# Gated DeltaNet sample step: state products moved from TensorE to VectorE, keys and queries broadcast through memory

## What is computed

```python
def sample_step(S, q, k, v, decay, beta):        # what the chunked rule comes to for one token
    delta = beta * (v - decay * (k @ S))         # 128 values
    S_new = decay * S + outer(k, delta)          # 128 x 128
    o = (q * 128 ** -0.5) @ S_new
    return o, S_new
```

## Time and profile before

| | us |
|---|---|
| median of three runs | 1199.55 |
| the three runs | 1198.0, 1199.55, 1202.51 |
| the profiled execution, its time | 1204.32 |
| the profiled execution, its span in the trace | 1202.5 |

### The profile page before, as it was taken

The page is one execution under the profiler, slowest core; times in us unless marked ns, Lnnn a source line. Parts: engine busy times, 40 slices in busy tenths (PEclk is TensorE's granted clock), DMA queues, the critical chain, the costliest instruction groups (busy, mean ns, idle before and its releaser), DMA issues. The chain is left out here.

```text
span 1202.5 us, 24731 instructions
## 1 busy us (share of the span) xinstructions
PE 1165.9 (97%) x8401; PEld 1087.4 (90%) x8401; DVE 801.4 (67%) x1987; ACT 475.1 (40%) x1216; POOL 307.2 (26%) x275
## 2 busy tenths in 40 slices
PE   5999999999999999999999999999999979999997
PEld 4899989998999899989988999899999979999996
DVE  5586567666766786777766766777776756565544
ACT  6453335434533444344434433453345335331211
POOL 0224112411242134122311241223122312222211
PEclk9999999999999999999999999999999999999999
DMA  7332455254525452635263525352535373423263
GB/s 249 93 98 73 145 158 162 72 165 147 168 64 177 136 162 62 203 110 166 67 193 108 168 66 194 116 161 81 182 111 168 93 251 129 150 88 101 73 212 143
DMA packets 83354, 164.18 MB, mean 137 GB/s; under 512 B 12801, under 2 KB 22882, under 8 KB 81698
## 3 DMA queue, kind: packets, MB, share of 16 engines
q1 hardware_dynamic: 81966, 161.47, 42.5%
q10 hardware_dynamic: 1312, 1.59, 0.5%
HBM read 144.78 MB, written 17.37 MB: 135 GB/s over the span
## 5 line engine op out<-in xcount | busy, mean ns | idle before, releaser
L643 PE MATMUL PJ<-h,w_hi 128*128 128x512 f32 x1110 | 419.3, 414 | 0.0
L1995 POOL TENSOR_TENSOR w_lo<-w_raw,w_hi 128x512 fp32r<-128x512 f32 x160 | 216.2, 1352 | 758.5 <-ACT w_hi L1035 758.1
L639 PE MATMUL PJ<-h,w_hi 128*128 128x264 f32 (+1 forms) x1216 | 358.0, 294 | 0.0
L640 PE MATMUL PJ<-h,w_hi 128*128 128x264 f32 (+1 forms) x1216 | 345.7, 284 | 0.0
L641 PE MATMUL PJ<-h,w_lo 128*128 128x264 f32 (+1 forms) x1216 | 345.4, 284 | 0.0
L644 PE MATMUL PJ<-h,w_lo 128*128 128x256 f32 x1110 | 311.3, 280 | 0.0
L643 PEld LDWEIGHTS PJ<-h,w_hi 128*128 128x128 f32 x1110 | 209.2, 188 | 42.8 <-DVE w_lo L1397 1.4
L640 PEld LDWEIGHTS PJ<-h,w_hi 128*128 128x128 f32 x1216 | 230.4, 189 | 2.2
L1035 ACT ACTIVATE w_hi<-w_raw 128x512 fp32r<-128x512 f32 x320 | 196.5, 623 | 86.4 <-PE PJ L641 79.1
L639 PEld LDWEIGHTS PJ<-h,w_hi 128*128 128x128 f32 x1216 | 230.0, 189 | 0.3
L641 PEld LDWEIGHTS PJ<-h,w_lo 128*128 128x128 f32 x1216 | 229.0, 188 | 0.0
(11 more groups left out here) (333 smaller groups left out, 1705.8 us busy)
## 6 DMA issues: line engine op xcount, KB each, us to landing
w_raw<-in_w_in SPq DMA_DIRECT2D x256, 256.0 KB, 2.7
w_raw<-in_w_out SPq DMA_DIRECT2D x64, 256.0 KB, 3.0
kvq<-in_cache_win_k SPq DMA_DIRECT2D x24, 512.0 KB, 5.0
kvq<-in_cache_win_v SPq DMA_DIRECT2D x24, 512.0 KB, 4.8
mem<-scratch_p SPq DMA_DIRECT2D x24, 512.0 KB, 5.7
out<-memx SPq DMA_DIRECT2D x16, 260.0 KB, 4.0
mem<-in_x_prompt SPq DMA_DIRECT2D x4, 1024.0 KB, 10.1
S<-in_state_delta SPq DMA_DIRECT2D x8, 512.0 KB, 5.8
```

The source lines that it names most:

```text
L639: pe.matmul(ps, wh, h_hi[:, k, tok], start=k == 0, stop=False)
L640: pe.matmul(ps, wh, h_lo[:, k, tok], start=False, stop=False)
L643: pe.matmul(both, wh, h2[:, :, k, tok], start=k == 0, stop=False)
L1995: pool.tensor_tensor(w_lo[:, par, 4 * q:4 * q + 4, :], w_raw[:, q, :, :], w_hi[:, par, 4 * q:4 * q + 4, :].bitcast(F32), ALU.subtract).the ...
```

## The change

The states are kept with the value dimension on the partitions and the key dimension along the row (the host transposes input and output; the DMAs keep their sizes). Then k @ S is a product along the row, and for that each partition needs the whole of k and of q of every sample:

- DVE transposes the samples' k columns into `qrow` in slot 15, SP writes them to memory with four small DMAs (`rows_to`) in slot 16 and reads them back in slot 19 as a broadcast to all partitions, `k_rows` (which lies in `gx`), 512 KB. The same for q: DVE slot 33, SP slot 35, broadcast to `q_rows` in slot 38.
- DVE does 8 fused multiply-and-sum instructions for k @ S in the slots 35 and 36, six small ones for delta in slot 37, 8 multiply-adds of 128 x 128 into `S0` in the slots 41 to 43, 8 fused ones for q @ S_new in the slots 44 to 47, and two small ones in slot 48. The last two follow in slot 51.
- PE keeps the sum of squares (slot 35, 16 columns) and the sum of o squared (slot 49). L910, L916 and L928 go. POOL keeps the scaling of `S0`, L2059 goes; so do L1747, L1748, L1763 to L1781 in their old form and L1795 on DVE, and one copy on ACT.
- The load of the first key block moves from slot 51 to slot 52, ahead of the q row's broadcast in the same slot; the products with the values on DVE move from the slots 47 to 50 to the slots 48 to 51.

```diff
             def attn_rows(h):
...
-                yield from idle(51)
+                yield from idle(52)
                 if not first:
                     sp.wait_ge(s["pv_ok"], h)
                 keys(0)
-                yield
-                sp.wait_ge(s["qrow_out"], 64 * h + 64)
+                sp.wait_ge(s["qrow_out"], 192 * h + 192)
                 sp.dma_start(qb[:], scratch_q[h].rearrange("b d -> (b d)").partition_broadcast(P)).then_inc(s["qb_in"], 16)
...
             # SP
             def delta_decode(h):
-                yield from idle(24)
+                yield from idle(16)
+                sp.wait_ge(s["q_row"], 3 * h + 1)
+                rows_to(scratch_dk[h])
+                yield from idle(3)
+                sp.wait_ge(s["qrow_out"], 192 * h + 64)
+                sp.dma_start(k_rows, scratch_dk[h].rearrange("b d -> (b d)").partition_broadcast(P)).then_inc(
+                    s["dk_in"], 16)
+                yield from idle(5)
                 if not isinstance(h, int) or h > 0:
                     sp.wait_ge(s["S0_out"], 16 * h)
+                    sp.wait_ge(s["d_vec"], h)
                 sp.dma_start(S0[:], state_delta[h]).then_inc(s["S0_in"], 16)
-                yield from idle(23)
-                sp.wait_ge(s["d_add"], 2 * h + 2)
-                sp.dma_start(st_s[0, :, h].rearrange("b d e -> d b e"), S0[:]).then_inc(s["S0_out"], 16)
+                yield from idle(11)
+                sp.wait_ge(s["q_row"], 3 * h + 2)
+                rows_to(scratch_dq[h])
+                yield from idle(2)
+                sp.wait_ge(s["d_ks"], h + 1)
+                yield
+                sp.wait_ge(s["qrow_out"], 192 * h + 128)
+                sp.dma_start(q_rows[:], scratch_dq[h].rearrange("b d -> (b d)").partition_broadcast(P)).then_inc(
+                    s["dq_in"], 16)
+                yield from idle(9)
+                sp.wait_ge(s["d_add"], h + 1)
+                sp.dma_start(st_s[0, :, h].rearrange("b e d -> e b d"), S0[:]).then_inc(s["S0_out"], 16)
...
             # PE
             def delta_decode(h):
...
-                pe.matmul(MD[:, 1, 0:24], ones[:], dd[:, 2:5, :].rearrange("p a b -> p (a b)"), start=True, stop=True)
-                for b in range(NB):
-                    last = pe.matmul(MD[:, 1, 32 + 2 * b:34 + 2 * b], S0[:, b, :], dd[:, 0:2, b], start=True,
-                                     stop=True)
+                pe.matmul(MD[:, 1, 0:16], ones[:], dd[:, 2:4, :].rearrange("p a b -> p (a b)"), start=True,
+                          stop=True).then_inc(s["d_sum"], 1)
+                yield from idle(14)
                 pe.wait_ge(s["d_vec"], h + 1)
-                for i in range(2):
-                    pe.transpose(MD[0:4 * NB, 1, i * P:(i + 1) * P], kv4[:, i, :], ident[:])
...
-                    pe.matmul(MD[:, 1, :], kvr_all[:, 0, :], vexp_all, start=True,
-                              stop=True).then_inc(s["d_outer"], 1)
...
             # DVE
+            def fused(x, rows, out, acc_, per):
+                for b in range(NB):
+                    last = dve.tensor_tensor_reduce(out=out[:, b * P:(b + 1) * P], in0=S0[:, b, :],
+                                                    in1=rows[:, b * P:(b + 1) * P], scale=1.0, scalar=0.0, op0=ALU.mult,
+                                                    op1=ALU.add, accum_out=acc_[:, b:b + 1])
+                    if b + 1 in per:
+                        yield
...
             def delta_decode(h):
...
+                dve.wait_ge(s["dk_in"], 16 * h + 16)
+                dve.wait_ge(s["S0_in"], 16 * h + 16)
+                yield from fused(s["d_ks"], k_rows, q_rows, dd[:, 0], (5,))
...
+                dve.wait_ge(s["S0_scaled"], h + 1)
+                for b in range(NB):
+                    last = dve.scalar_tensor_tensor(S0[:, b, :], k_rows[:, b * P:(b + 1) * P], dd[:, 4, b:b + 1],
+                                                    S0[:, b, :], ALU.mult, ALU.add)
+                    if b in (2, 4):
+                        yield
+                last.then_inc(s["d_add"], 1)
...
+                dve.wait_ge(s["dq_in"], 16 * h + 16)
+                yield from fused(None, q_rows, q_rows, dd[:, 1], (3, 5, 6))
...
-            def attn_decode(hh, late=0, gap=31, each=2):
+            def attn_decode(hh, late=0, gap=32, each=2):
```

More of the change, by code:

```diff
@@ L491, in conv_out, with rows_to @@
                     yield from idle(8)
+            def rows_to(scratch):
+                for i in range(HD // 32):
+                    sp.dma_start(scratch[:, 32 * i:32 * i + 32], qrow[32 * i + 32 - NB:32 * i + 32, :]).then_inc(
+                        s["qrow_out"], 16)
             def attn_out(h):
                 yield from idle(47)
[L496 to L499, removed]
+                sp.wait_ge(s["q_row"], 3 * h + 3)
+                rows_to(scratch_q[h])
                 yield from idle(6)
@@ L1287, in delta_decode @@
                 rsqrt(dd[:, 9:11, :], MD[:, 1, 0:2 * NB].rearrange("p (a b) -> p a b", a=2), 1.0, s["d_rs"])
[L1288 to L1292, removed]
+                yield from idle(13)
+                act.wait_ge(s["d_sq"], h + 1)
+                rsqrt(dd[:, 10, :], MD[:, 1, 16:24], 1.0 / HD, s["d_rs2"])
             def attn_decode(hh, late=0):
@@ L1539, in own_a @@
                 dve.wait_ge(s["q_ok"], h + 1)
-                if not first:
-                    dve.wait_ge(s["qrow_out"], 64 * h)
+                dve.wait_ge(s["qrow_out"], 192 * h + 128)
                 dve.transpose(qrow[:], xa[:, TT - 32:TT]).then_inc(s["q_row"], 1)
@@ L1740, in delta_decode @@
             def delta_decode(h):
+                first = isinstance(h, int) and h == 0
                 kd, qd = xk[:, TP:TT], cq[:, TP:TT]
-                yield from idle(33)
+                yield from idle(15)
+                dve.wait_ge(s["kv_silu"], 2 * h + 1)
+                if not first:
+                    dve.wait_ge(s["qrow_out"], 192 * h)
+                dve.transpose(qrow[:], xk[:, TT - 32:TT]).then_inc(s["q_row"], 1)
+                yield from idle(18)
                 dve.wait_ge(s["q_silu"], h + 1)
-                dve.wait_ge(s["kv_silu"], 2 * h + 2)
@@ L1745, in delta_decode @@
-                if isinstance(h, int) and h == 0:
+                if first:
                     dve.wait_ge(s["gates_act"], 5)
-                dve.tensor_copy(dd[:, 0, :], kd)
-                dve.tensor_copy(dd[:, 1, :], qd)
                 dve.tensor_tensor(dd[:, 2, :], kd, kd, ALU.mult)
-                dve.tensor_tensor(dd[:, 3, :], qd, qd, ALU.mult)
+                dve.tensor_tensor(dd[:, 3, :], qd, qd, ALU.mult).then_inc(s["dkq"], 1)
+                dve.wait_ge(s["qrow_out"], 192 * h + 64)
@@ L1772, in delta_decode @@
-                link(dve.tensor_tensor(dd[:, 7, :], dd[:, 7, :], rq, ALU.mult))
-                dve.tensor_tensor(dd[:, 8, :], dd[:, 7, :], dd[:, 7, :], ALU.mult).then_inc(s["d_vec"], 1)
-                yield from idle(3)
-                dve.wait_ge(s["d_rows_ok"], h + 1)
-                kvh = kvr.bitcast(F32)
-                link(dve.scalar_tensor_tensor(kvl[:], kvh, -2.0,
-                                              MD[0:4 * NB, 1, 0:2 * P].rearrange("p (a d) -> p a d", a=2), ALU.mult,
-                                              ALU.add))
@@ L1780, in delta_decode @@
-                for i in range(2):
-                    dve.scalar_tensor_tensor(kvr[:, i, :], kvl[:, i, :], terms[:, NB + i:NB + i + 1], kvh[:, i, :],
-                                             ALU.mult, ALU.add).then_inc(s["d_terms"], 1)
+                yield
+                yield
+                dve.wait_ge(s["dk_in"], 16 * h + 16)
+                dve.wait_ge(s["S0_in"], 16 * h + 16)
+                yield from fused(s["d_ks"], k_rows, q_rows, dd[:, 0], (5,))
+                yield
+                dve.wait_ge(s["d_ks"], h + 1)
@@ L1789, in delta_decode @@
                                          ALU.mult).then_inc(s["gated_bd"], 1)
-                for n in range(2):
-                    yield from idle(n + 1)
-                    dve.wait_ge(s["d_outer"], 2 * h + n + 1)
-                    dve.wait_ge(s["S0_scaled"], h + 1)
-                    st = S0[:, 4 * n:4 * n + 4, :]
-                    dve.tensor_tensor(st, st, MD[:, 1, :].rearrange("p (b e) -> p b e", b=4), ALU.add).then_inc(
-                        s["d_add"], 1)
             def bt_s(n):
@@ L2050, in delta_decode @@
                 yield from idle(37)
[L2051 removed]
+                pool.wait_ge(s["d_ks"], h + 1)
                 pool.tensor_tensor(S0[:], S0[:], dd[:, 11, :].unsqueeze(2).to_broadcast((P, NB, P)),
                                    ALU.mult).then_inc(s["S0_scaled"], 1)
[L2054 to L2064 removed]
             pool.wait_ge(s["memset_ok"], 1)
```

106 lines of the change are left out of this document (36 added, 70 removed).

## The result

The changed kernel took 1208.42 us in the median (1207.26 to 1208.7, four runs), the kernel before 1198.78 us (1197.85 to 1202.51, four runs) on the same chip: 1.0073 times as long, 95% interval 1.0054 to 1.0091. That is 9.6 us more, where 3 more were forecast: inside the range of 1187 to 1217 us, outside the forecast's own of 1194 to 1206.

The account below looks back on a forecast made before the run. PE, 97% busy, was taken as the bound, with DVE's and the loads' lateness able to hurt by place. Heads 1 to 7 +3.5, head 0 -2.2, clock +1.7: +3 us on 1199.55, so 1202.5 us, range 1187 to 1217.

Parts of the forecast that it names:

- rival 2: Waits at the head's end halve the clock in all seven heads: 1212.7 us; chance 0.36 together with slower sums.
- the slower sums: Sums of the terms slower than the forecast's own range of 1194 to 1206 us; chance 0.36 together with rival 2.
- What leaves PE: L910, L916 and L928 go from PE: 2.75 us a head, 22.0 us in eight (20.4 to 24.7).
- DVE in all: DVE's total work rises by about 2 to 3 us a head of 118, no bound by itself.
- Slots 20 to 24: Four DMA issues ahead of store L490 delay DVE's L1428 and L1618; PE waits 0.5 us in heads 1 to 7.
- Slots 35 to 46: Products come out even; three ahead of L1683 in slot 45 cost PE 0.15 us a head (0 to 1).
- Slots 50 to 54: Products with the values in slot 51 make DVE about 1.2 us later at L1688; PE waits 0.9 us.
- Slots 52 to 59: Q row queued behind the keys lands later; 2.6 us reach PE by the head's end (1.3 to 3.5).
- Head 0: DVE idle at this head's end, so only 0.4 us lost there; the head gains, rounded, 2.2 us.
- The clock: One more stretch at half clock after a wait at a head's end, as in head 4: +1.7 us.
- Its second way to that price: Lateness of 3.5 us at the head's end and 1 us in slot 45: 7 x 1.75 = 12.2 us.
- Rival 1: PE's gain arrives whole, 1177.5 us (chance 0.08), or in part, 1188.8 us (chance 0.14).

Follow-up runs that it names:

- the two runs that took them away: Changed kernel, keys in slot 51, multiply-adds one slot earlier: 1188.87 us; that plus da in slot 53 and query products 1 and 4 in slots 44, 45: 1182.08 us.
- the last kernel: Changed kernel with keys in slot 51, da in slot 53, multiply-adds from slot 40, query products 1 and 4 in slots 44 and 45: 1182.08 us.
- the added matmuls: Changed kernel with eight unused small matmuls more on PE: in slot 35 1223.17 us, in slot 57 1207.63 us.
- all four reorderings: Changed kernel with keys in slot 51, da instructions in slot 53, multiply-adds from slot 40, two query products moved later in slots 44 and 45: 1182.08 us.

## Why the prediction was right or wrong

- **The range held, the forecast did not.** The time is 9.6 us over before, where +3 was forecast, within -6 to +6. It lies nearest to rival 2 and the slower sums (0.36). The mechanism, lateness of DVE and of the q row that PE pays at the head's end, is the forecast's; two of its terms were mis-sized.
- **What leaves PE: right.** The slots 34 to 50 are 2.07 us shorter, with new waits in the slots 43 and 46 inside, worth 0.29 and 0.31 us by the two runs that took them away. With both gone the last kernel has 2.65, against 2.75. That such time counts one for one there is shown by the added matmuls.
- **DVE in all: right in sign, too small.** 25.0 us more in 8 heads are 3.1 a head; 2 to 3 were forecast. PE's busy time fell by 15.2 us, where some 20 were named as a sign. The fused products cost 0.21 us start to start as taken.
- **Slots 20 to 24: wrong, nothing instead of 0.5 us in the heads 2 to 6.** The store L480 (before L490) was indeed issued late, at 430.58, behind four `scratch_dk` issues of 1.74 us, and DVE waited as forecast:

```profile
432.13 0.69 DVE L1419 TENSOR_REDUCE memx<-PJ 128x256 f32<-128x512 f32 x1 [3.37 <-DMA out<-memx]
...
433.81 0.69 DVE L1607 TENSOR_TENSOR memx<-memx 128x520 f32<-128x520 f32 x1
```

  The forecast said 432.25 for L1419. What failed is the step behind it. The forecast held that time against PE's times of before, but in this kernel the head begins 0.67 us later (393.15, before 392.48), and PE with it. And L1607 (before L1618) took 0.69 us and not the 1.2 that were left to it. The result was there at 434.50 and PE came for it at 434.88, without a wait. Head 1 paid 0.3 us and head 7 2.1 (a wait of 1.8). Together that is 2.4 of the 3.5 us forecast, near by luck: why these two heads pay is not shown.
- **Slots 35 to 46: mis-sized, 0.6 us instead of 0.15.** The prediction gave the multiply-adds no surcharge, since POOL's scaling of `S0` is over by slot 41. POOL's `w_lo` at 467.24 was overlooked. It adds 1.05 us to three instructions, of which 0.3 reached PE. The other 0.3 is slot 46, where the products of the queries stand ahead of L1672; 0.15 was the estimate. Beside POOL's scaling of `S0` (1.90 us) no product ran late enough to matter: a `w_lo` of DVE took 2.00 us there, where it had taken 1.51 before, and the slots 37 and 38 of PE are as before.
- **Slots 50 to 54: right.** 0.78 us of wait, forecast 0.9; the slot itself is 1.05 us longer. Counted from PE's start of slot 50, L1677 begins 1.17 us later than L1688 did, where 1.2 were forecast.
- **Slots 52 to 59: right in mechanism, 0.3 to 2.2 us too small, 1.0 in the mean.** This is the term that missed most. The forecast put the landing 4.8 + 1.5 = 6.3 us behind the issue of the keys. Measured are 7.0 us in head 3 (491.80 to 498.82): the keys' own issue holds the q row's back by 0.5, which the sum left out, and from its issue the q row then took 6.5. Counted from PE's start of slot 50 the first product begins 3.3 us later than before, where 2.6 were forecast. DVE's wait for the row rose from 0.66 to 2.98 us. The 2.6 us by the head's end are 2.75 in the old kernel with the moves alone, and 2.9 to 4.8 in the changed one. The chain named behind it (L1705, ACT, POOL, SP, the third key block, L1715) did not give it back. Its two parts don't simply add: undoing the keys alone takes 1.9 to 3.7 us off this stretch, 2.6 in the mean, undoing the values alone 0.4, which slot 49 takes back.
- **Head 0: wrong, -0.2 us instead of -2.2.** Its stretch from slot 50 on grew by 1.5 us where 0.4 were taken: the q row behind the keys holds this head too, for with the keys in slot 51 it is back at 26.05. That DVE had less to do here did not help against a landing. Its slots 34 to 50 gained 1.73, since its wait at L843 was 0.87.
- **The clock: the item of +1.7 did not come.** By the granted clock the wait of 2.26 us at the end of head 4 has full clock behind it. Past head 0, and without the last 5 us, where both kernels are at half clock, there are 6.8 us at half clock, where before had 10.2 (631.0 to 634.4 and 989.4 to 996.2). One of these stretches is new, from 983.2 on, behind a wait for L1686 in slot 59 of head 7. PE's timeline:

```profile
632.32 0.71 PE L764 MATMUL MX<-memx 128*128 128x128 f32 x3 [2.26 <-DVE gB L1704]
...
982.45 0.38 PE L874 MATMUL MX<-small,mem 128*128 128x128 f32 x1 [1.76 <-DVE small L1686]
```

and busy times by stretch (PE, PEld, DVE, ACT, POOL), then the granted clock, DMA share and GB/s:

```profile
631.00:634.40 3.40, 2.08 (x12) 1.85 (x13) 3.20 (x19) 0.00 (x0) 0.00 (x0) 1.00 0.10 40
983.20:986.60 3.40, 3.40 (x18) 3.40 (x17) 2.98 (x16) 0.68 (x3) 1.36 (x1) 0.50 0.98 363
```

  Before, a wait of 2.02 us in the same place was followed by 0.50. So rival 2 came nearer with 1212.7 us than the forecast with 1202.5, by luck, for its reason was seen once and not in seven heads. Its second way to that price, a lateness of 3.5 us at the head's end and 1 us in slot 45, is nearer to what happened: 3.6 us in the mean and 0.6 in the slots 43 and 46.
- **Rival 1 (the gain arrives).** In the changed kernel it did not, but reordering brought most of it: 9.7 us of it come with the keys in slot 51 (1199.68 to 1190.02), 16.9 with all four reorderings (1199.02 to 1182.08). The Trainium skill (Perfetto Trace Analysis, Identifying the Most-Contended Engine) says to optimize first the engine with the highest occupancy. Here PE was that engine (97% busy, its weight loads 90%). Taken alone, the step did not pay (PE 15.2 us less busy, 9.6 us slower); it did once the queues had been put in order.

In sum, over the forecast: 6.1 us from slot 50 on in the heads 1 to 6, 3.7 in the slots 34 to 50 of seven heads, 2.0 in head 0. Under it: 2.6 in head 7, whose lateness cost nothing, 1.1 in the slots 20 to 24, and the clock's 1.7. That makes 6.4 of the 6.6 us between forecast and measurement; without the last three the miss would have been 12.

## What to carry to other kernels

In this kernel, work taken from the busiest engine counts fully where that engine's own pace sets the others', and not at all where a load and another engine's queue end the stretch; a few dummy instructions in each place tell which. Look at small reorderings that come with a big change first: one 512 KB load, issued directly ahead of another load that is waited for, cost 18.4 us, nearly as much as the change took off PE (21, as 8 times 2.65). On an engine that serves a critical one in order, put what nobody waits for behind the result that somebody does.

## What was unexpected of the hardware

- A broadcast load of 512 KB takes 5.0 us when only 256 KB were issued in the microsecond ahead of it, and 6.5 us when 256 and 512 KB were. In the 4.2 us before the slower one's traffic the queue moved nothing (14 slices of the DMA view).
- A multiply-add of 128 x 128 with two inputs from SBUF grows from 0.35 to 1.40 us beside POOL's 128 x 512 subtraction; a `w_lo` of DVE grows from 0.68 to 1.15 us (at 432.7), and to 2.00 beside POOL's scaling of `S0`, and a fused product of 128 x 128 from 0.29 to 1.37 us.
- PE stood still for 2.26 us before a stretch with full clock and for 2.02 us before one with half. In slot 59 of head 7 it stood for 1.76 us before half clock in the changed kernel, and a slot on for 1.84 us before full clock in the kernel before. The length of the wait alone doesn't tell which comes.
